# Depthwise convolution on two engines: GpSimd makes the taps of half of its tiles

## The chip, the cores and the metric

One core of a Trainium2 chip runs the whole program. The metric is device time in microseconds (us) of that core, the median of several executions. A core has five engines with their own instruction streams, which meet only through semaphores: PE (TensorE, matmuls), DVE (VectorE), ACT (ScalarE), POOL (GpSimd) and SP (SyncE, which here only starts DMAs). On-chip memory (SBUF) has 128 partitions; matmuls write to PSUM, 8 banks of 128 x 512 float32.

## The reference

Two transformer-like blocks over 256 tokens of width 1024, batch 1, all in float32. The first block has a layer whose mixer is a state space branch beside a neighbourhood attention, then an MLP, an mLSTM layer and a second MLP; the second block mixes three branches, then cross attention and a gated MLP. Every product multiplies the 256 tokens by weights that are read once. The part that the change touches is the first step of the state space branch, over 1536 channels (1024 for x, 256 each for B and C):

```python
proj = h @ w_in
z, xbc, dt_raw, qkv = jnp.split(proj, [s1, s2, s3], axis=-1)
...
xbc = jax.nn.silu(centred_dwconv(xbc, conv_w, conv_b))      # 5 taps, one filter per channel
xs, bm, cm = jnp.split(xbc, [SSD_WIDTH, SSD_WIDTH + SSD_GROUPS * SSD_STATE], axis=-1)
```

## The kernel before, in words

**Products.** The stream of weights comes from device memory in chunks of 128 x 2048 float32 (1 MB), through a ring of 7 slots that SP fills. For each chunk ACT rounds the weights to a high part (`split_hi`, L1382, into one of 3 buffers `w_hi`), DVE subtracts to get the low part in place (`split_lo`, L1393), and PE makes three passes (L1058: high x high, high weights x low source, low weights x high source). A group is 512 columns of output, two chunks at 1024 input rows, and goes to one pair of PSUM banks. When it is complete, ACT takes one bank and DVE the other. `in0` is the first product; its groups 0, 1 and 2 are the 1536 channels of the convolution (B and C first, then x), groups 3 and 4 are q, then k, z and v.

**Woven work.** Each engine's program is a Python generator. `Woven` runs the main product one quarter of a chunk at a time, and after each quarter lets side threads advance to a step given by `paced` tables. So the order of instructions on each engine is fixed when the program is built; nothing is reordered at run time. DVE has another side job in these stages, the guests: products of one vector with weights (the modulation `cond @ ada_w`), a multiply-add of 128 x 512 per row of tiles (L1200), whose sums PE then turns by four small matmuls (L1019). PE waits in order for the guest's last multiply-add before it goes on with the product.

**The convolution.** Channels lie on partitions, 12 tiles of 128 channels, tokens along the free dimension. `xp` holds the projection with two columns of padding at either side, `xc` the result. For each of the three groups of 4 tiles: ACT makes the first tap and the bias (`scalar`, L2202, 4 instructions, mark `first_tap`); DVE makes the other four taps of the 4 tiles, 16 instructions of the form `xc = xp[shifted] * w + xc` (`vector`, L2254, mark `convolved`), one tap after the other with a wait on its own steps between taps; ACT then applies Silu to the 4 tiles in one instruction (L2213, mark `silu_in`). In ACT's stream a Silu is followed by what the product needs: taking a group out of PSUM (L1991, L1998), splitting the next chunk (L1382), the first taps of the next group (L2202), and the high part of the running sums of the step sizes (L2065) that DVE's L2102 waits for.

**Readers of the convolution.** PE's L2140 (the product of B and C) reads the tiles of group 0, L2154 (transposes of x) those of groups 1 and 2. `silu_in` releases them.

**GpSimd.** In this stage POOL starts two DMAs (L594, L596) and then is idle until the next stages. It computes only in the second block: 16 times the four instructions L3207, L3208, L3210 (tensor times a scalar, 128 x 256) and L3212 (difference of two tensors, 128 x 256) for the phases of the S5 branch, and L3514 and L3519 (two tensors, 128 x 1024).

**Memory.** `e` is a ring of three buffers of 768 columns for the decays of the scan, used after the convolution. Before that `tmp`, its first 5 x 256 columns, holds the step sizes.

Of the kernel before, what the change touches and what calls it, by code (L numbers as in the profile page):

```python
# [300 lines left out]
class Mark:  # L301


    def __init__(self, sem, before):
        self.sem, self.before = sem, before
# [170 lines left out]
class Stage:  # L476
# [11 lines left out]
    def vector(self, dve, st):  # L488
        pass

    def gpsimd(self, pool, st):
        pass
# [1620 lines left out]
class Ssd(Stage):  # L2113
# [5 lines left out]

    def __init__(self, k, xp, xc, xt, cb, cs4, bias, tmp, e, in0):
        super().__init__(k)
        self.xp, self.xc, self.xt, self.cb, self.cs4, self.bias = xp, xc, xt, cb, cs4, bias
        self.tmp, self.e, self.first, self.narrow_in = tmp, e, in0.first_group, in0.narrow_in()
        self.m = {n: k.mark(n, c) for n, c in (
            ("biased", 1), ("log_in", 1), ("rates_in", 1), ("steps_in", 1), ("log_steps_in", 1), ("sums_in", 2),
            ("sums_hi", 1), ("sums_lo", 1), ("offsets_in", 1), ("offsets_turned", 1), ("offsets_taken", 1),
            ("first_tap", 3), ("convolved", 3), ("silu_in", 3), ("cb_in", 2), ("cb_taken", 2), ("x_turned", 4), ("x_taken", 4),
            ("decay_args", 2 * NH), ("decays_in", 2 * NH), ("weights_in", NH), ("head_out", NH), ("head_taken", NH // 2))}  # L2130

    def tensor(self, pe):
# [62 lines left out]
    def scalar(self, act, st):  # L2195
        k, m = self.k, self.m
        for n in range(3):
            at = 4 * ((n + 2) % 3)
            act.wait_ge(k.act_took, k.act_groups[self.first + n + 1])
            act.wait_ge(k.dve_took, k.dve_groups[self.first + n + 1])  # L2200
            for j in range(at, at + 4):
                ins = act.activation(self.xc[:, j, :], self.xp[:, j, 0:TOK], ACT.Identity,  # L2202
                                     scale=k.par("conv_w")[:, j:j + 1], bias=k.par("conv_b")[:, j:j + 1])
            ins.then_inc(m["first_tap"].sem, 1)
            yield
            if n == 2:
                for g in range(2):
                    act.wait_ge(*m["cb_in"].at(g + 1))
                    act.activation(self.cb[:, g, :], k.ps[:, 4 + g, :], ACT.Identity).then_inc(m["cb_taken"].sem, 1)
            for _ in range(4):  # L2210
                yield
            act.wait_ge(*m["convolved"].at(n + 1))
            act.activation(self.xc[:, at:at + 4, :], self.xc[:, at:at + 4, :], ACT.Silu).then_inc(m["silu_in"].sem, 1)  # L2213
            yield
            if n == 0:
                yield
        for half in range(2):
            for t in range(TT):
                act.wait_ge(*m["x_turned"].at(2 * half + t + 1))
                act.activation(self.xt[:, t, 512 * half:512 * half + 512], k.ps[:, 4 + t, :], ACT.Identity) \  # L2220
                   .then_inc(m["x_taken"].sem, 1)
            yield
        act.wait_ge(*m["offsets_taken"].at(1))
        for h in range(NH):
            e = self.e[:, h % 3, :]
            act.wait_ge(*m["decay_args"].at(2 * h + 1))
            if h >= 3:
                act.wait_ge(*m["head_out"].at(h - 2))
            c = h
            act.activation(e[:, 0:TOK], k.ps[:, 4, 0:TOK], ACT.Exp, bias=self.bias[:, 0, c:c + 1])  # L2230
            act.activation(e[:, 3 * P:4 * P], k.ps[:, 4, TOK:3 * P], ACT.Exp, bias=self.bias[:, 1, c:c + 1]) \
               .then_inc(m["decays_in"].sem, 1)
            yield
            act.wait_ge(*m["decay_args"].at(2 * h + 2))
            c = 64 + h
            act.activation(e[:, 4 * P:5 * P], k.ps[:, 5, 0:P], ACT.Exp, bias=self.bias[:, 0, c:c + 1])
            act.activation(e[:, 2 * P:3 * P], k.ps[:, 5, P:2 * P], ACT.Exp, bias=self.bias[:, 1, c:c + 1])
            act.activation(e[:, 5 * P:6 * P], k.ps[:, 5, 2 * P:3 * P], ACT.Exp, bias=self.bias[:, 1, c:c + 1]) \
               .then_inc(m["decays_in"].sem, 1)
            yield  # L2240
        yield

    def vector(self, dve, st):
        k, m = self.k, self.m
        for n in range(3):
            at = 4 * ((n + 2) % 3)
            for tap in range(5):
                if tap == 1:
                    dve.wait_ge(*m["first_tap"].at(n + 1))
                elif tap > 1:  # L2250
                    st.wait()
                for j in range(at, at + 4) if tap else ():
                    src, w = self.xp[:, j, tap:tap + TOK], k.par("conv_w")[:, 12 * tap + j:12 * tap + j + 1]
                    ins = dve.scalar_tensor_tensor(self.xc[:, j, :], src, w, self.xc[:, j, :], ALU.mult, ALU.add)  # L2254
                    if tap < 4 or j < at + 3:
                        st(ins)
                    else:
                        ins.then_inc(m["convolved"].sem, 1)
                yield
            yield  # L2260
            if n == 0:
                yield
        yield
        yield

        def weigh(h):
            e = self.e[:, h % 3, :]
            dve.wait_ge(*m["decays_in"].at(2 * h + 2))
            both = e[:, 0:6 * P].rearrange("p (a c) -> p a c", c=P)
            st(dve.tensor_tensor(both[:, 0:4:3, :], both[:, 0:4:3, :], both[:, 4:6, :], ALU.add))  # L2270
            st.wait()
            dve.tensor_tensor(e[:, 0:2 * TOK], e[:, 0:2 * TOK], self.cb[:, h // 8, :], ALU.mult) \
               .then_inc(m["weights_in"].sem, 1)

        def take(p):
            dve.wait_ge(*m["head_out"].at(2 * p + 2))
            dve.scalar_tensor_tensor(self.xc[:, p, :], self.xc[:, p, :], k.par("d_skip")[:, p:p + 1],
                                     k.ps[:, 6, 0:TOK], ALU.mult, ALU.add).then_inc(m["head_taken"].sem, 1)

        dve.wait_ge(*m["cb_taken"].at(2))  # L2280
        for h in range(NH):
            yield
            weigh(h)
            if h >= 2 and h % 2 == 0:
                take(h // 2 - 1)
            yield
        take(NH // 2 - 1)
        yield
# [2075 lines left out]
def all_stages(k, bias, kept, kept_hi):  # L4364
# [53 lines left out]
    mem = MemGroups(k, mem_turn, mem_rates, kept_hi, kept, mem_his, mem_lo, region(k, at_m).take(TT, CN))  # L4418
    tables = BiasLoad(k, table, bias, mem_turn, mem_rates)
    in0 = in0_stage(k, xp, xc, zs, qT, kT, v, z_in, ada_take(k, mods), first_norm, mem_turn.stored)  # L4420
    ssd = Ssd(k, xp, xc, xt, cb, cs4, biases, tmp, e, in0)
    norm = SsdNorm(k, xc[:, 0:KD, :], zs, ring2(at_z, KD, TOK, True), ring2(at_x, KD, TOK, True), rows, in0, z_in)
    na = Neighbours(k, lambda h, t: qT[64 * (h % 2):64 * (h % 2) + 64, h // 2, t * P:(t + 1) * P],
                    lambda h: kT[64 * (h % 2):64 * (h % 2) + 64, h // 2, :],
# [157 lines left out]
```

## Time and profile before

| | |
|---|---|
| median of 3 runs | 1630.98 us (1630.41 to 1633.61) |
| the profiled execution | 1631.24 us, span of its profile 1629.4 us |
| mean granted TensorE clock | 0.974 of full speed |
| PE busy, PE weight loads | 1529.9 us (94%), 1316.0 us |
| DVE busy | 1149.6 us (71%) |
| ACT busy | 789.2 us (48%) |
| POOL busy | 83.6 us (5%) |

The span is the time from the first to the last instruction of one profiled execution. "Busy" counts the time in which an engine had an instruction in work, also if that instruction waited for data or for a port. Shares over the whole span say little of one stage; the rows further down are taken from the stage that the change touches, about 70 to 130 us after the start.

### The profile page before, as it was taken

What the parts mean: (1) busy time and instruction counts of PE and PEld (TensorE: products, weight loads), DVE (VectorE), ACT (ScalarE), POOL (GpSimd) and SP (SyncE); (2) the same over time, 40 slices, a digit from 0 to 9 for tenths busy, and PEclk for the clock granted to TensorE, in tenths of its full rate; (3) what the DMA queues carried; (4) which work ended last, traced back from release to release, by engine and by line L of the source; (5) the groups of instructions that cost most, each with busy time, mean ns of one, the idle gap of its engine ahead of it and who ended that gap; (6) DMA issues with size and microseconds to landing.
All of it is one profiled execution on the core that took longest, in us unless ns stands there. A gap on an engine that the chain in (4) does not pass through costs nothing.

```text
span 1629.4 us, 23049 instructions
## 1 busy us (share of the span) xinstructions
PE 1529.9 (94%) x9240; PEld 1316.0 (81%) x9240; DVE 1149.6 (71%) x1812; ACT 789.2 (48%) x1078; POOL 83.6 (5%) x82
## 2 busy tenths in 40 slices
PE   8789998989999999999999999889998899999998
PEld 8779876679988888887899888756774778789987
DVE  4896775589877766776787567999963775466653
ACT  3645645454433546444554435656533734444442
POOL 0000000000000000000000002940020000000000
PEclk7889999999999999999999999999999999999999
DMA  9854523468777654335566555323321434145551
GB/s 389 318 220 185 215 85 136 144 225 318 283 280 288 243 169 145 131 128 194 200 240 233 181 195 206 130 104 111 125 103 75 181 129 155 59 172 184 181 190 68
DMA packets 42377, 298.10 MB, mean 183 GB/s; under 512 B 4640, under 2 KB 4896, under 8 KB 7328
## 3 DMA queue, kind: packets, MB, share of 16 engines
q1 hardware_dynamic: 39840, 283.00, 47.3%
q0 software_dynamic: 1568, 8.39, 1.4%
q10 hardware_dynamic: 864, 5.24, 0.9%
q8 instruction: 75, 1.23, 0.3%
q14 instruction: 30, 0.25, 0.0%
HBM read 292.42 MB, written 4.19 MB: 182 GB/s over the span
## 4 chain that ended last, share of the span: by engine, by line
PE 46%; DVE 22%; PEld 14%; issue 8%; ACT 7%; DMA 1%; POOL 1%; PEldq 1%; ACTq 0%; DVEq 0%; SPq 0%; POOLq 0%
PE ps L1050 16%; PE ps L1058 15%; PEld ps L1050 8%; DVE ring_at_lo L1393 7%; PEld ps L1058 5%; ACT w_hi L1382 3%; PE ps L1099 2%; DVE arena_at L1200 2%; DMA ring_at<-stream 1%; DVE arena_at L2254 1%; PE ps L2688 1%; PE ps L1274 1%; DVE arena_at L3255 1%; PE ps L546 1%; DVE arena_at L3264 1%
## 5 line engine op out<-in xcount | busy, mean ns | idle before, releaser
L1393 DVE TENSOR_TENSOR ring_at_lo<-ring_at,w_hi 128x2048 fp32r<-128x2048 f32 (+1 forms) x218 | 496.2, 2278 | 173.6 <-ACT w_hi L1382 173.1
L1382 ACT ACTIVATE w_hi<-ring_at 128x2048 fp32r<-128x2048 f32 (+1 forms) x218 | 413.7, 1902 | 193.9 <-PE ps L1050 134.0
L1050 PE MATMUL ps<-w_hi,arena_at_lo 128*128 128x512 f32 x1104 | 304.5, 397 | 1.9 <-DVEq L4504 0.8
L1058 PE MATMUL ps<-h_hi,w_hi 128*128 128x256 f32 x1440 | 244.3, 293 | 8.5 <-ACT w_hi L1382 3.4
L1050 PEld LDWEIGHTS ps<-w_hi,arena_at_lo 128*128 128x128 f32 x1104 | 204.3, 188 | 49.6 <-issue 3.0
L1058 PE MATMUL ps<-hT_at_lo,w_hi 128*128 128x256 f32 x1440 | 232.7, 285 | 0.0
L1058 PE MATMUL ps<-h_hi,ring_at_lo 128*128 128x256 f32 x1440 | 227.0, 280 | 0.0
L1058 PEld LDWEIGHTS ps<-h_hi,w_hi 128*128 128x128 f32 x1440 | 202.5, 194 | 15.8 <-issue 10.9
L1058 PEld LDWEIGHTS ps<-hT_at_lo,w_hi 128*128 128x128 f32 x1440 | 201.6, 193 | 0.0
L1058 PEld LDWEIGHTS ps<-h_hi,ring_at_lo 128*128 128x128 f32 x1440 | 194.7, 191 | 0.0
L1050 PE MATMUL ps<-ring_at_lo,arena_at_lo 128*128 128x512 f32 x552 | 172.1, 393 | 0.0
L1050 PE MATMUL ps<-w_hi,h_hi 128*128 128x512 f32 x368 | 124.5, 419 | 0.0
L1050 PEld LDWEIGHTS ps<-ring_at_lo,arena_at_lo 128*128 128x128 f32 x552 | 103.7, 188 | 24.3
L1050 PE MATMUL ps<-w_hi,hT_at_lo 128*128 128x512 f32 x368 | 116.0, 397 | 0.0
L1050 PE MATMUL ps<-ring_at_lo,h_hi 128*128 128x512 f32 x368 | 116.0, 396 | 0.0
L1200 DVE SCALAR_TENSOR_TENSOR arena_at<-ring_at,cond,arena_at 128x512 f32<-128x512 f32 x140 | 104.8, 748 | 3.7 <-DVE arena_at L1200 0.5
L1050 PEld LDWEIGHTS ps<-w_hi,hT_at_lo 128*128 128x128 f32 x368 | 70.3, 191 | 16.2
L1050 PEld LDWEIGHTS ps<-ring_at_lo,h_hi 128*128 128x128 f32 x368 | 69.6, 189 | 16.1
L1050 PEld LDWEIGHTS ps<-w_hi,h_hi 128*128 128x128 f32 x368 | 65.6, 191 | 19.5 <-issue 8.7
L546 PE MATMUL ps<-con 128*128 128x256 f32 x134 | 34.9, 412 | 8.3 <-DMA con<-consts 4.4
L546 PEld LDWEIGHTS ps<-con 128*128 128x128 f32 x134 | 27.0, 206 | 14.3 <-DMA con<-consts 4.4
L1099 PE MATMUL ps<-w_hi,arena_at_lo 128*128 128x512 f32 x128 | 35.5, 399 | 2.5 <-DVEq L4504 1.6
(471 smaller groups left out, 1743.6 us busy)
## 6 DMA issues: line engine op xcount, KB each, us to landing
ring_at<-stream SPq DMA_DIRECT2D x266, 1024.0 KB, 4.8
arena_at_lo<-kept_hi POOLq DMA_DIRECT2D x4, 1024.0 KB, 7.0
arena_at<-bias ACTq DMA_DIRECT2D x4, 768.0 KB, 5.8
kept<-arena_at POOLq DMA_DIRECT2D x4, 512.0 KB, 4.6
arena_at<-kept ACTq DMA_DIRECT2D x2, 1024.0 KB, 7.6
x_res<-x SPq DMA_DIRECT2D x1, 1024.0 KB, 9.5
arena_at<-mem POOLq DMA_DIRECT2D x1, 1024.0 KB, 11.1
kept_hi<-arena_at_lo POOLq DMA_DIRECT2D x1, 1024.0 KB, 4.2
```

What stands on the lines that cost most here:

```text
L546: pe.matmul(k.ps[:, bank, 0:TOK], k.con("ident"), k.con("ones"), start=True, stop=True)
L1050: mm = pe.matmul(k.ps[:, bank + t, :], x_tile(f, slice(t * P, (t + 1) * P)), w, start=first and n == 0, stop=last and n == 2)
L1058: mm = pe.matmul(k.ps[:, bank + q // 2, (q % 2) * TOK:(q % 2 + 1) * TOK], w[:, q * P:(q + 1) * P], x, start=first and n == 0 and q % 2 == ...
L1099: mm = pe.matmul(k.ps[:, bank + t, :], x[:, f, t * P:(t + 1) * P], w, start=f == 0 and n == 0, stop=f == KD - 1 and n == 2)
L1200: ins = dve.scalar_tensor_tensor(acc, w, cond, acc, ALU.mult, ALU.add)
L1274: pe.matmul(k.ps[:, self.opening_bank(n), 2 * q:2 * q + 2], k.ring[:, c % RING, kk, q * P:(q + 1) * P], k.cond[:, CK * j + kk:CK * j + kk ...
L1382: act.activation(k.w_hi[:, s % HI, 0:n, :], k.ring[:, c % RING, 0:n, :], ACT.Identity).then_inc(k.hi_done, 1)
L1393: dve.tensor_tensor(k.w_lo[:, c % RING, 0:n, :], k.ring[:, c % RING, 0:n, :], k.w_hi[:, s % HI, 0:n, :].bitcast(F32), ALU.subtract).then_i ...
L2254: ins = dve.scalar_tensor_tensor(self.xc[:, j, :], src, w, self.xc[:, j, :], ALU.mult, ALU.add)
L2688: mm = pe.matmul(k.ps[:, 6 + t, 0:MDV + 2], a, b, start=j == 0, stop=j == len(parts) - 1)
L3255: dve.tensor_tensor_scan(self.g[:, at], mag, a[:, at], 0.0, ALU.mult, ALU.add) \
L3264: dve.tensor_tensor(halves(self.b2[:, i % 3, :]), halves(self.g)[:, ::-1, :], halves(self.sn[:, i % 3, :])[:, ::-1, :], ALU.mult).then_inc ...
```

## The change

DVE makes taps 1 to 4 of the first two tiles of each group only. POOL makes those of the other two: it makes each product by `tensor_scalar` into a buffer `taps` (two tiles of 128 x 256), waits for both, and adds both to `xc` by one `tensor_tensor` of 128 x 512. `taps` lies in `e` behind `tmp`. ACT's Silu waits for both engines.

```diff
@@ Ssd
             ("first_tap", 3), ("convolved", 3), ("taps_by_pool", 36), ...
@@ Ssd.scalar
             act.wait_ge(*m["convolved"].at(n + 1))
+            act.wait_ge(*m["taps_by_pool"].at(12 * n + 12))
             act.activation(self.xc[:, at:at + 4, :], self.xc[:, at:at + 4, :], ACT.Silu).then_inc(m["silu_in"].sem, 1)
@@ Ssd.gpsimd
+    def gpsimd(self, pool, st):
+        k, m = self.k, self.m
+        for n in range(3):
+            at = 4 * ((n + 2) % 3)
+            pool.wait_ge(*m["first_tap"].at(n + 1))
+            for tap in range(1, 5):
+                done = 12 * n + 3 * tap - 3
+                if done:
+                    pool.wait_ge(*m["taps_by_pool"].at(done))
+                for j in (at + 2, at + 3):
+                    src, w = self.xp[:, j, tap:tap + TOK], k.par("conv_w")[:, 12 * tap + j:12 * tap + j + 1]
+                    pool.tensor_scalar(self.taps[:, j - at - 2, :], src, w, 1.0, ALU.mult, ALU.mult) \
+                        .then_inc(m["taps_by_pool"].sem, 1)
+                pool.wait_ge(*m["taps_by_pool"].at(done + 2))
+                pool.tensor_tensor(self.xc[:, at + 2:at + 4, :], self.xc[:, at + 2:at + 4, :], self.taps, ALU.add) \
+                    .then_inc(m["taps_by_pool"].sem, 1)
@@ Ssd.vector
-                for j in range(at, at + 4) if tap else ():
+                for j in range(at, at + 2) if tap else ():
                     src, w = self.xp[:, j, tap:tap + TOK], k.par("conv_w")[:, 12 * tap + j:12 * tap + j + 1]
                     ins = dve.scalar_tensor_tensor(self.xc[:, j, :], src, w, self.xc[:, j, :], ALU.mult, ALU.add)
-                    if tap < 4 or j < at + 3:
+                    if tap < 4 or j < at + 1:
                         st(ins)
@@ all_stages
-    ssd = Ssd(k, xp, xc, xt, cb, cs4, biases, tmp, e, in0)
+    ssd = Ssd(k, xp, xc, xt, cb, cs4, biases, tmp, e, in0, region(k, at_e + 5 * TOK).take(2, TOK))
```

Line numbers shift by 19 behind the new function: DVE's taps are L2273 in the changed kernel. POOL's new stream, from the second DMA on (the first tap of group 0 and part of the second; the pattern repeats 12 times):

```order
7 L596 DMA kept_hi<-arena_at_lo 128x2048 [waits turned_hi]
8 L2256 ISA
9 L2256 TENSOR_SCALAR arena_at<-arena_at,par 128x256 [waits first_tap]
10 L2256 TENSOR_SCALAR arena_at<-arena_at,par 128x256
11 L2259 TENSOR_TENSOR arena_at<-arena_at 128x512 [waits taps_by_pool]
12 L2256 TENSOR_SCALAR arena_at<-arena_at,par 128x256 [waits taps_by_pool]
```

Each addition waits for the products before it, and each tap's first product for the addition before it. ACT's stream around the first two Silus, before (L2213) and in the changed kernel (L2215):

```order
53 L2213 ACT_TABLE_LOAD
54 L2213 ACTIVATE arena_at<-arena_at 128x1024 [waits convolved]
55 L1382 ACTIVATE w_hi<-ring_at 128x2048 [waits chunk_used,chunk_loaded5]
56 L2202 ACTIVATE arena_at<-arena_at,par 128x256 [waits dve_took_group,act_took_group]
57 L2202 ACTIVATE arena_at<-arena_at,par 128x256 x3
```

```order
53 L2215 ACT_TABLE_LOAD [waits taps_by_pool]
54 L2215 ACTIVATE arena_at<-arena_at 128x1024 [waits convolved]
55 L1382 ACTIVATE w_hi<-ring_at 128x2048 [waits chunk_used,chunk_loaded5]
56 L2203 ACTIVATE arena_at<-arena_at,par 128x256 [waits dve_took_group,act_took_group]
57 L2203 ACTIVATE arena_at<-arena_at,par 128x256 x3
58 L1382 ACTIVATE w_hi<-ring_at 128x2048 [waits chunk_used,chunk_loaded6]
59 L2215 ACTIVATE arena_at<-arena_at 128x1024 [waits taps_by_pool,convolved]
60 L1991 ACTIVATE arena_at<-ps 128x2x256 [waits chunk_used]
61 L2065 ACTIVATE arena_at_lo<-arena_at 128x512 [waits sums_in]
```

The order on ACT is the same; the load of Silu's table, which had no wait, now stands behind the wait for POOL. On DVE the order around the third group's last taps, before and now (only the count in a tap differs):

```order
97 L2254 SCALAR_TENSOR_TENSOR arena_at<-arena_at,par 128x256 x4
98 L1200 SCALAR_TENSOR_TENSOR arena_at<-ring_at,cond,arena_at 128x512
99 L1393 TENSOR_TENSOR ring_at_lo<-ring_at,w_hi 128x2048
100 L1200 SCALAR_TENSOR_TENSOR arena_at<-ring_at,cond,arena_at 128x512
101 L2002 TENSOR_SCALAR arena_at<-ps 128x512
```

```order
97 L2273 SCALAR_TENSOR_TENSOR arena_at<-arena_at,par 128x256 x2
98 L1200 SCALAR_TENSOR_TENSOR arena_at<-ring_at,cond,arena_at 128x512
99 L1393 TENSOR_TENSOR ring_at_lo<-ring_at,w_hi 128x2048
100 L1200 SCALAR_TENSOR_TENSOR arena_at<-ring_at,cond,arena_at 128x512
101 L2002 TENSOR_SCALAR arena_at<-ps 128x512
```

The `L1200` at 100 is the guest's last step, for which PE's L1019 waits.

## Rows read from the trace of the kernel before

**Rows 1.** Page, part 1: busy us (share of the span) xinstructions.

```profile
PE 1529.9 (94%) x9240; PEld 1316.0 (81%) x9240; DVE 1149.6 (71%) x1812; ACT 789.2 (48%) x1078; POOL 83.6 (5%) x82
```

**Rows 2.** Windows: PE, PEld, DVE, ACT, POOL busy (x), PEclk, DMA share, GB/s.

```profile
72.00:119.00 47.00, 39.49 (x297) 38.92 (x296) 46.42 (x84) 23.02 (x26) 0.00 (x0) 0.90 0.63 236
119.00:170.00 51.00, 50.63 (x383) 45.80 (x384) 36.13 (x49) 28.99 (x62) 0.00 (x0) 0.95 0.47 170
```

**Rows 3.** Groups by line, 71.8 to 119.2 us: xcount | busy us, mean ns | idle.

```profile
L2254 DVE SCALAR_TENSOR_TENSOR arena_at<-arena_at,par 128x256 f32<-128x256 f32 x48 | 20.0, 478 | 0.1
L1393 DVE TENSOR_TENSOR ring_at_lo<-ring_at,w_hi 128x2048 fp32r<-128x2048 f32 x6 | 13.7, 2286 | 0.7 <-ACT w_hi L1382 0.6
```

**Rows 4.** Timeline of DVE: start us, us, engine, line, op, [idle before].

```profile
84.57 2.31 DVE L1200 SCALAR_TENSOR_TENSOR arena_at<-ring_at,cond,arena_at 128x512 f32<-128x512 f32 x3
86.98 2.29 DVE L1393 TENSOR_TENSOR ring_at_lo<-ring_at,w_hi 128x2048 fp32r<-128x2048 f32 x1
93.25 5.09 DVE L2254 SCALAR_TENSOR_TENSOR arena_at<-arena_at,par 128x256 f32<-128x256 f32 x12
101.84 1.40 DVE L2102 TENSOR_TENSOR arena_at_lo<-arena_at,arena_at_lo 32x512 fp32r<-32x512 f32 x2
105.07 1.67 DVE L2254 SCALAR_TENSOR_TENSOR arena_at<-arena_at,par 128x256 f32<-128x256 f32 x4
```

**Rows 5.** Timeline of ACT, first taps, Silus and what stands behind them.

```profile
69.78 2.06 ACT L2202 ACTIVATE arena_at<-arena_at,par 128x256 f32<-128x256 f32 x4
80.96 1.28 ACT L2213 ACT_TABLE_LOAD   x1
84.08 1.07 ACT L2213 ACTIVATE arena_at<-arena_at 128x1024 f32<-128x1024 f32 x1 [1.84 <-DVE arena_at L2254]
85.05 1.90 ACT L1382 ACTIVATE w_hi<-ring_at 128x2048 fp32r<-128x2048 f32 x1
98.38 1.06 ACT L2213 ACTIVATE arena_at<-arena_at 128x1024 f32<-128x1024 f32 x1 [7.67 <-DVE arena_at L2254]
99.82 0.62 ACT L2065 ACTIVATE arena_at_lo<-arena_at 128x512 fp32r<-128x512 f32 x1
101.51 2.08 ACT L2202 ACTIVATE arena_at<-arena_at,par 128x256 f32<-128x256 f32 x4 [1.07 <-DVE arena_at L1995]
115.70 1.06 ACT L2213 ACTIVATE arena_at<-arena_at 128x1024 f32<-128x1024 f32 x1 [7.28 <-DVE arena_at L2254]
```

**Rows 6.** Timeline of PE, the two waits for DVE and the second transposes.

```profile
90.08 1.59 PE L1019 MATMUL ps<-ones,arena_at 128*128 128x2 f32 x8 [1.64 <-DVE arena_at L1200]
119.34 1.83 PE L1019 MATMUL ps<-ones,arena_at 128*128 128x2 f32 x8 [6.21 <-DVE arena_at L1200]
126.41 1.04 PE L2154 MATMUL ps<-con,arena_at 128*128 128x128 f32 x8
```

**Rows 7.** Groups by line, POOL, whole span: xcount | busy us, mean ns.

```profile
L3208 POOL TENSOR_SCALAR arena_at<-con,arena_at 128x256 f32<-128x256 f32 x16 | 22.7, 1417 | 0.0
L3207 POOL TENSOR_SCALAR arena_at<-con,arena_at 128x256 f32<-128x256 f32 x16 | 15.8, 988 | 4.7 <-ACT arena_at L3186 3.4
L3212 POOL TENSOR_TENSOR arena_at<-arena_at 128x256 f32<-128x256 f32 x16 | 18.3, 1144 | 1.3
```

**Rows 8.** Instructions of one line: ns min/median/max, first and last start.

```profile
L3207 POOL TENSOR_SCALAR arena_at<-con,arena_at x16: 474/732/2614, 1010.3 to 1080.4; 128x256 f32<-128x256 f32 x16
L3212 POOL TENSOR_TENSOR arena_at<-arena_at x16: 727/986/2649, 1018.5 to 1082.3; 128x256 f32<-128x256 f32 x16
L3514 POOL TENSOR_TENSOR arena_at<-arena_at x2: 1889/2858/3826, 1202.3 to 1206.1; 128x1024 f32<-128x1024 f32 x2
```

**Rows 9.** The same of a DVE line, from 1009 to 1085 us.

```profile
L3246 DVE TENSOR_TENSOR arena_at<-arena_at x9: 659/898/1162, 1026.0 to 1082.7; 128x512 f32<-128x512 f32 x9
```

**Rows 10.** Timelines of POOL and DVE around 1035 us.

```profile
1034.91 2.65 POOL L3212 TENSOR_TENSOR arena_at<-arena_at 128x256 f32<-128x256 f32 x1
1034.48 2.48 DVE L1393 TENSOR_TENSOR ring_at_lo<-ring_at,w_hi 128x2048 fp32r<-128x2048 f32 x1
```

More of the change, by code:

```diff
@@ L2113, with __init__ @@
 class Ssd(Stage):
-    def __init__(self, k, xp, xc, xt, cb, cs4, bias, tmp, e, in0):
+    def __init__(self, k, xp, xc, xt, cb, cs4, bias, tmp, e, in0, taps):
         super().__init__(k)
+        self.taps = taps
         self.xp, self.xc, self.xt, self.cb, self.cs4, self.bias = xp, xc, xt, cb, cs4, bias
@@ L2128, in __init__ @@
             ("sums_hi", 1), ("sums_lo", 1), ("offsets_in", 1), ("offsets_turned", 1), ("offsets_taken", 1),
-            ("first_tap", 3), ("convolved", 3), ("silu_in", 3), ("cb_in", 2), ("cb_taken", 2), ("x_turned", 4), ("x_taken", 4),
+            ("first_tap", 3), ("convolved", 3), ("taps_by_pool", 36), ("silu_in", 3), ("cb_in", 2), ("cb_taken", 2), ("x_turned", 4), ("x_taken", 4),
             ("decay_args", 2 * NH), ("decays_in", 2 * NH), ("weights_in", NH), ("head_out", NH), ("head_taken", NH // 2))}
```

## The prediction

> **What bounds the kernel now.** I read the page's busy times first: PE is busy for 94% of the span, POOL for 5% [rows 1]. That makes POOL look free, and says nothing of the 50 us in which the convolution runs. So the next view is busy time by stretch: from 72 to 119 us DVE is busy for 46.4 of 47 us, PE only for 39.5 and ACT for 23.0; from 119 us on PE is busy for 50.6 of 51 us and DVE for 36.1 [rows 2]. DVE sets the pace first, PE afterwards, and PE's two idle times in the first stretch, 1.64 us before 90.08 and 6.21 us before 119.34, both end with DVE's L1200 [rows 6]. The chain of waits says the same in order of time: it runs along DVE up to the guest's last step and crosses to PE at 119.3 us. What DVE does there is in the groups by line: 48 taps (20.0 us), 6 low splits (13.7 us) [rows 3], and between them guest steps (L1200). All three read two tensors from SBUF.
>
> ACT is not the bound there, but it has little room. It waits 1.84, 7.67 and 7.28 us for DVE before the three Silus [rows 5], and what stands behind the first two is wanted almost at once: DVE's split at 86.98 follows ACT's L1382, which ends at 85.05 + 1.90 = 86.95 [rows 4, 5], with DVE done with its guest steps at 86.88; DVE's L2102 at 101.84 needs ACT's L2065, which ends at 99.82 + 0.62 = 100.44 [rows 4, 5].
>
> **What is taken from DVE.** Twelve taps in a row take 5.09 us, 0.42 each [rows 4]. 24 of 48 go: 24 x 0.42 = 10.1 us, 3.4 us in each group. The waits between taps stay.
>
> **What POOL's work takes by itself.** Per group and tap two products and an addition of 128 x 512. A product of 128 x 256 takes 0.47 us at least, an addition 0.73 at 256 columns and 1.89 at 1024 [rows 8], so 1.51 ns a column and 1.11 us at 512. With the two handovers a tap takes 2.2 us, a group 8.8. But while DVE works beside it POOL's instructions are longer: means of 0.99 and 1.42 us for the products, 1.14 for the addition of 256 [rows 7], so some 1.5 for one of 512. Then a tap takes 4.1 us and a group 16.4. What these instructions waited for can be read at 1035 us: POOL's addition begins at 1034.91 while DVE's split runs from 1034.48 to 1036.96, takes 2.65 us in place of 0.73, and ends 0.6 us behind the split [rows 10]. POOL's instruction is in work but held until DVE's ends. Here DVE is as full of such instructions as there, but a tap (0.42 us) stands in front of POOL for less time than S5's instructions (0.66). I take **3.8 us a tap, 15.2 a group**, near the upper end, and keep 2.2 and 4.5 as bounds. The library call before POOL's first product I cost at nothing: the same call stood before L3207, whose longest instance, 2.61 us, is explained by one split in front.
>
> **What POOL's work costs DVE.** The other direction is in the row of L3246, which reads two SBUF tensors: 0.66 us undisturbed, 0.90 typically beside POOL's products, 1.16 at most beside an addition of 256 columns [rows 9]. The same split as above takes 2.48 us, against 2.28 alone, a product of POOL having been ahead of it [rows 3, 10]. So a product holds DVE up for 0.24 us, an addition of 256 for 0.50, and one of 512 by the slope above for 0.50 + 0.39 = 0.89. Per tap 1.37 us, 12 taps 16.4 us if every instruction meets such an instruction of DVE. That is more than the 10.1 us that DVE sheds. The Trainium skill (SBUF — State Buffer, "SBUF: two separate sides") calls the pair of ports that the two engines share an exclusive lock that the winner has "for the whole instruction". The trace agrees that there is no sharing, but not on the length: DVE lost 0.24 us to instructions that take 0.47. By the page's rule a tap would cost DVE 0.47 + 0.47 + 1.11 = 2.05 us; I go by the rows.
>
> **Group by group.** *First group.* The first taps end at 69.78 + 2.06 = 71.84 us, and the Silu ran 12.2 us later, at 84.08 [rows 5]. POOL is done at 71.84 + 15.2 = 87.0. In front of this Silu stands a load of its table, 1.28 us, which lay in ACT's wait at 80.96 [rows 5] and now comes behind the wait for POOL. So the Silu starts at 88.3, 4.2 us late, and with it the split, DVE's L1393, the guest step that PE waits for, and the first taps of the next group, which end at 93.1 in place of 86.95 + 2.06 = 89.0. DVE alone would have been at that split at 86.9 - 3.4 + 5.5 = 89.0, before ACT's 91.2: ACT sets the time.
> *Second group.* POOL: 93.1 + 15.2 = 108.3, against a Silu at 98.38. L2065 ended 2.06 us behind the Silu's start [rows 5], so it ends at 110.3, where DVE needed it at 101.84: DVE, which has been through its taps for long, stands still and resumes **8.5 us late**. The first taps of the third group come at about 112.4 (the 1.07 us that ACT waited for DVE in front of them is gone), DVE's own taps at 105.07 + 8.5 = 113.6.
> *Third group.* From there to the guest's last step DVE sheds 3.4 us. POOL gets through some three taps meanwhile; since part of its instructions meet an instruction on PSUM or none, I charge 2.5 taps, 3.4 us, with 0 and 5.5 as bounds. So the guest's last step and PE's L1019 come 8.5 us late. POOL itself ends near 128, the Silu near 129; PE's second L2154, its reader, stood at 126.41 [rows 6] and now stands at 135: hidden, and it stays so up to 21 us a group.
>
> Sum: +4.2 (first group) + 4.3 (second) - 3.4 + 3.4 = **+8.5 us**. From 119 us on PE has no idle time to take it in [rows 2], and a ring of 7 chunks can't save up more than it holds, so the shift goes through to the end. The profiled execution took 1631.24 us, 0.26 above the median of the runs: 1639.7 against it, **1639.5 us** as a median. Of the clock: PE was granted 0.90 of full speed from 72 to 119 us and 0.95 after [rows 2]; it idles before L1019 in both kernels, so I add no term, but 2 us to either side.
>
> **Rivals.**
> *DVE's relief wins (0.09).* If POOL's reads and DVE's did not hold each other up, POOL would need 8.8 us a group, less than the 12.2, 9.5 and 12.2 us from first taps to Silu. DVE would shed 10.1 us, but PE has no idle time between 91.5 and 113 us, so of the first two groups' relief only PE's 1.64 us come back, and of the third's all 3.4: -5.0, 1626.0 us. For it: PE's waits all end with DVE, and POOL is empty. Against it: rows 9 and 10.
> *A draw on DVE (0.14).* POOL's additions hold the ports no longer than for 256 columns, and its chain stays inside ACT's waits. DVE alone decides: -10.1 + 24 x 0.24 + 12 x 0.50 = +1.7, with the table's load up to +3.0: 1632.7 to 1634. Against it: the second group has only 9.5 us, and POOL's means don't fit into that.
> *The whole instruction is held (0.12).* Then a tap costs DVE 0.68 us more, 8.2 us in all, of which two thirds fall on time that counts: 8.5 + 5.5, 1645 us. This is what the rule of the page above would do here.
> The decisive point between faster and slower is POOL's time for a group: over some 10 us the second Silu is late, and L2065 hands that to DVE.
>
> **How the numbers follow.** My forecast (1634.5 to 1643) has 0.62, the rivals 0.09, 0.14 and 0.12; 0.03 is left for POOL at over 4.5 us a tap, beyond 1646. About 0.2% (3.3 us) can be told from no change. The draw is mostly within that and gives 0.11 of "same"; slower has 0.80. The range from 1632 to 1646 takes in the draw, the forecast and the whole-instruction case, and leaves out the faster one.
>
> **What would show it.** Right: POOL's 36 instructions take about 45 us, the products 0.8 to 1.4 us and the additions 1.4 to 1.6; DVE's taps are longer than 0.48 us in the mean; ACT's waits before the Silus end with POOL; the table's load starts only when POOL is done; DVE has idle time before L2102 that ends with ACT's L2065, and PE's L1019 stands near 128. Wrong: POOL's products near 0.47 us and additions near 1.1 (the first rival), or DVE without idle time before L2102 (the draw).

## The result and the profile after

| | before | after |
|---|---|---|
| median, us | 1631.22 (20 runs, 1626.67 to 1633.77) | 1635.53 (20 runs, 1632.79 to 1643.55) |
| after / before | | 1.0039, 95% interval 1.0028 to 1.0051 |
| profiled execution, us | 1631.24, span 1629.4 | 1632.88, span 1631.0 |

The change costs 0.39%, that is 6.4 us, 4.6 to 8.3 us by the interval. It is slower, as forecast, inside the range and 4 us below the number. The medians differ by only 4.3 us, since eight of the 20 executions after lie at 1639.8 to 1643.6 us, apart from the other twelve (up to 1636.7) and at a slightly lower mean granted clock.

The page's busy times after, against [rows 1]: POOL has 36 instructions and 36 us more, DVE has 24 instructions fewer and is busy for 6.6 us longer.

```profile
PE 1524.1 (93%) x9237; PEld 1312.3 (80%) x9240; DVE 1156.2 (71%) x1788; ACT 789.6 (48%) x1078; POOL 120.0 (7%) x118
```

Groups of instructions by line, the shapes kept apart, DVE of the changed kernel from 71 to 122 us (count | busy us, mean ns | idle before). L2273 are the taps, L1200 the guest's steps.

```profile
L2273 DVE SCALAR_TENSOR_TENSOR arena_at<-arena_at,par 128x256 f32<-128x256 f32 x24 | 22.9, 992 | 0.1
L1393 DVE TENSOR_TENSOR ring_at_lo<-ring_at,w_hi 128x2048 fp32r<-128x2048 f32 x5 | 11.4, 2284 | 1.4 <-ACT w_hi L1382 1.4
L1200 DVE SCALAR_TENSOR_TENSOR arena_at<-ring_at,cond,arena_at 128x512 f32<-128x512 f32 x12 | 10.4, 867 | 0.1
```

**24 taps now keep DVE busy for longer (22.9 us) than 48 did (20.0) [rows 3].** The work was halved and the time per tap doubled. The low splits have not changed (2.28 us). The two groups of POOL over the stretch, products and additions:

```profile
L2256 POOL TENSOR_SCALAR arena_at<-arena_at,par 128x256 f32<-128x256 f32 x24 | 20.4, 859 | 19.9 <-ACT arena_at L2203 19.0
L2259 POOL TENSOR_TENSOR arena_at<-arena_at 128x512 f32<-128x512 f32 x12 | 16.9, 1410 | 1.0
```

PE's two waits for the guest, which stood at 90.08 and 119.34 with 1.64 and 6.21 us of idle time [rows 6]:

```profile
93.06 1.84 PE L1019 MATMUL ps<-ones,arena_at 128*128 128x2 f32 x8 [4.49 <-DVE arena_at L1200]
126.69 1.84 PE L1019 MATMUL ps<-ones,arena_at 128*128 128x2 f32 x8 [9.14 <-DVE arena_at L1200]
```

ACT: the first taps of the second and third group (L2203), and the three Silus (L2215) with the load of their table, to be compared with [rows 5]:

```profile
85.55 1.28 ACT L2215 ACT_TABLE_LOAD   x1 [4.47 <-POOL arena_at L2259]
86.85 1.06 ACT L2215 ACTIVATE arena_at<-arena_at 128x1024 f32<-128x1024 f32 x1
89.62 2.06 ACT L2203 ACTIVATE arena_at<-arena_at,par 128x256 f32<-128x256 f32 x4
103.23 1.06 ACT L2215 ACTIVATE arena_at<-arena_at 128x1024 f32<-128x1024 f32 x1 [9.75 <-DVE arena_at L2273]
106.36 2.08 ACT L2203 ACTIVATE arena_at<-arena_at,par 128x256 f32<-128x256 f32 x4 [1.07 <-DVE arena_at L1995]
123.05 1.06 ACT L2215 ACTIVATE arena_at<-arena_at 128x1024 f32<-128x1024 f32 x1 [9.77 <-DVE arena_at L2273]
```

Only the first Silu waits for POOL. The other two wait for DVE, as before.

How DVE loses its time is best read in the third group. The timeline of DVE in the changed kernel ("..." stands for lines left out; the last line is the guest's last step, behind POOL's end):

```profile
117.13 0.96 DVE L1200 SCALAR_TENSOR_TENSOR arena_at<-ring_at,cond,arena_at 128x512 f32<-128x512 f32 x1
118.02 2.10 DVE L2273 SCALAR_TENSOR_TENSOR arena_at<-arena_at,par 128x256 f32<-128x256 f32 x2
120.04 0.96 DVE L1200 SCALAR_TENSOR_TENSOR arena_at<-ring_at,cond,arena_at 128x512 f32<-128x512 f32 x1
120.92 2.10 DVE L2273 SCALAR_TENSOR_TENSOR arena_at<-arena_at,par 128x256 f32<-128x256 f32 x2
...
125.80 0.74 DVE L1200 SCALAR_TENSOR_TENSOR arena_at<-ring_at,cond,arena_at 128x512 f32<-128x512 f32 x1
```

The timeline of POOL over the same microseconds:

```profile
117.03 1.42 POOL L2256 TENSOR_SCALAR arena_at<-arena_at,par 128x256 f32<-128x256 f32 x2
118.52 1.30 POOL L2259 TENSOR_TENSOR arena_at<-arena_at 128x512 f32<-128x512 f32 x1
119.93 1.42 POOL L2256 TENSOR_SCALAR arena_at<-arena_at,par 128x256 f32<-128x256 f32 x2
121.43 1.31 POOL L2259 TENSOR_TENSOR arena_at<-arena_at 128x512 f32<-128x512 f32 x1
```

The two engines go step by step: three instructions of POOL fit three of DVE. The guest's step takes 0.96 us in place of 0.74, and the two taps 2.10 in place of some 0.84 (0.42 each [rows 4]). The line for all taps says how the 2.10 divides (minimum, median and maximum in ns):

```profile
L2273 DVE SCALAR_TENSOR_TENSOR arena_at<-arena_at,par x24: 472/696/1516, 74.4 to 121.5; 128x256 f32<-128x256 f32 x24
```

One tap of a pair waits behind a product (696 ns, 0.22 more than 0.478), the other behind an addition (1516 ns, 1.04 more). The guest's step in front of them waits behind the other product, 0.22 us. So one tap on POOL, of two tiles, costs DVE 0.22 + 0.22 + 1.04 = 1.48 us in this group, 5.9 us for four, and takes 8 x 0.42 = 3.4 us off it: 2.5 us net.

### The profile page after: what moved, and what is told of

Read it like the earlier page. It is cut to its first block, busy times and chain, and to the rows that moved or that the text cites. A ratio compares the mean times of both kernels' runs of the same rounds, so it can differ in the third digit from the quotient of the medians.

```text
span 1631.0 us, 23063 instructions
## 1 busy us (share of the span) xinstructions
PE 1524.1 (93%) x9237; PEld 1312.3 (80%) x9240; DVE 1156.2 (71%) x1788; ACT 789.6 (48%) x1078; POOL 120.0 (7%) x118
## 4 chain that ended last, share of the span: by engine, by line
PE 47%; DVE 22%; PEld 14%; issue 8%; ACT 7%; DMA 1%; POOL 1%; PEldq 1%; ACTq 0%; DVEq 0%; SPq 0%; POOLq 0%
PE ps L1050 17%; PE ps L1058 15%; PEld ps L1050 8%; DVE ring_at_lo L1393 7%; PEld ps L1058 5%; ACT w_hi L1382 3%; DVE arena_at L1200 2%; PE ps L1099 2%; DVE arena_at L2273 1%; PE ps L2707 1%; PE ps L1274 1%; DMA ring_at<-stream 1%; PE ps L3177 1%; DVE arena_at L3274 1%; PE ps L546 1%
## 5 line engine op out<-in xcount | busy, mean ns | idle before, releaser
L1050 PE MATMUL ps<-w_hi,arena_at_lo 128*128 128x512 f32 x1104 | 304.5, 397 | 1.8 <-DVEq L4523 0.8
L1058 PEld LDWEIGHTS ps<-h_hi,w_hi 128*128 128x128 f32 x1440 | 201.1, 193 | 16.9 <-issue 11.6
L1200 DVE SCALAR_TENSOR_TENSOR arena_at<-ring_at,cond,arena_at 128x512 f32<-128x512 f32 x140 | 106.3, 759 | 3.4
L1019 PE MATMUL ps<-ones,arena_at 128*128 128x2 f32 x160 | 22.2, 261 | 21.6 <-DVE arena_at L1200 21.6
## 6 DMA issues: line engine op xcount, KB each, us to landing
arena_at<-mem POOLq DMA_DIRECT2D x1, 1024.0 KB, 11.1
```

Source lines behind the costliest of these rows:

```text
L1019: mm = pe.matmul(k.ps[:, ADA, 2 * q:2 * q + 2], k.guest_acc[:, n % 2, q * P:(q + 1) * P], k.ones[:, :], start=True, stop=True)
L1050: mm = pe.matmul(k.ps[:, bank + t, :], x_tile(f, slice(t * P, (t + 1) * P)), w, start=first and n == 0, stop=last and n == 2)
L1058: mm = pe.matmul(k.ps[:, bank + q // 2, (q % 2) * TOK:(q % 2 + 1) * TOK], w[:, q * P:(q + 1) * P], x, start=first and n == 0 and q % 2 == ...
L1200: ins = dve.scalar_tensor_tensor(acc, w, cond, acc, ALU.mult, ALU.add)
```

## The experiments

The first two take the change apart: the relief without POOL's work, and POOL's work without the relief. Two more take the Silus' waits away and halve POOL's share. Two give POOL one kind of instruction only, and the rest ask where the lost time goes and how to avoid it. The edits are shown against the changed kernel, those of `delay`, `guest_at_9` and `guests_at_6_9` against the kernel before; "..." marks what is left out. "Shift" is always the start of PE's second L1019 against 119.34 us. The profiles start the stretch up to 0.3 us apart (the first taps of ACT at 69.47 us in the changed kernel, 69.78 before, 69.92 at the latest), so shifts are good to some 0.3 us. Ratios are to the kernel before, run beside each set on the same chip (medians 1629.81, 1631.08 and 1630.41 us for the three sets).

### `relief_only`: what DVE sheds, by itself

```diff
-            act.wait_ge(*m["taps_by_pool"].at(12 * n + 12))
...
-    def gpsimd(self, pool, st):
...
```

> Left out: taps 1 to 4 of the last two tiles of each group; nobody makes them. DVE has 24 taps, POOL none. This prices DVE's relief alone. PE's second wait for the guest (L1019) ended at 119.3 us before and at 126.7 us in the changed kernel. Ports theory (each POOL instruction holds up DVE's, and DVE is the bound): without POOL the relief of 10.1 us is cut by PE's own pace to about 5: L1019 near 114.5, the time about 5 us below the kernel before. Waits theory (the loss comes from ACT waiting for POOL's chain and the table's load behind it): the same here, so this run only fixes what is to be gained.

Measured: 1623.68 us, ratio 0.996 (0.9943 to 0.9977), which is worth 3.7 to 9.3 us less. The second L1019 stands at 111.51 us:

```profile
111.51 1.49 PE L1019 MATMUL ps<-ones,arena_at 128*128 128x2 f32 x8 [3.00 <-DVE arena_at L1200]
```

A shift of -7.8 us, not the -5 that I expected. The relief is real and it reaches PE. What the changed kernel lost is thus 7.8 + 7.35 = 15.2 us against this one.

### `beside`: POOL's work without any relief

```diff
-            act.wait_ge(*m["taps_by_pool"].at(12 * n + 12))
...
-                pool.tensor_tensor(self.xc[:, at + 2:at + 4, :], self.xc[:, at + 2:at + 4, :], self.taps, ALU.add) \
+                pool.tensor_tensor(self.taps, self.xp[:, at + 2:at + 4, 0:TOK], self.taps, ALU.add) \
...
-                for j in range(at, at + 2) if tap else ():
+                for j in range(at, at + 4) if tap else ():
```

> DVE makes all 48 taps as before. POOL does its 24 products and 12 additions beside it, into a buffer that nothing reads, and no Silu waits for it (only ACT's later writes over the same memory do). Ports theory: DVE loses 1.3 to 1.4 us for each of the 12 taps that POOL works on, 15 us or somewhat more: L1019 near 134, the time 12 to 16 us above before. Waits theory: nothing waits for POOL, so L1019 stays at 119 to 120 and the time is that of before.

Measured: 1650.2 us, ratio 1.012 (1.0099 to 1.0141). No Silu waits for POOL's 36 instructions, and yet PE's waits for DVE between 70 and 170 us are three times those of the kernel before, which were 7.9 us in all. The two largest groups (us in total, times, longest):

```profile
PE ps L1019 <- DVE arena_at L1200: 14.2, 2, 8.9
PE ps L1058 <- DVE ring_at_lo L1393: 7.9, 3, 3.5
```

The shift is 136.21 - 119.34 = +16.9 us, where I expected 15 or somewhat more. The time rose by 16.1 to 23 us, above the 12 to 16 that I expected; what came on top of the shift was not traced. DVE does exactly the work of before, so all of it is time in which its instructions were in work and held:

```profile
L2273 DVE SCALAR_TENSOR_TENSOR arena_at<-arena_at,par 128x256 f32<-128x256 f32 x48 | 30.5, 693 | 0.1
L1393 DVE TENSOR_TENSOR ring_at_lo<-ring_at,w_hi 128x2048 fp32r<-128x2048 f32 x7 | 17.0, 2435 | 0.7 <-ACT w_hi L1382 0.6
L1200 DVE SCALAR_TENSOR_TENSOR arena_at<-ring_at,cond,arena_at 128x512 f32<-128x512 f32 x14 | 13.2, 943 | 0.1
```

Against the kernel before the taps take 10.5 us more, the guest steps 14 x 0.2 = 2.8 and the splits 7 x 0.15 = 1.1; most of the remaining 2.5 us is in L2084 and L2089, which are some 1.0 us longer each. The forecast's term, 16.4 us for 12 taps of POOL, is confirmed as a size.

### `unwaited`: is it the wait?

The first two edits of `beside` without the third: DVE keeps its two tiles.

```diff
-            act.wait_ge(*m["taps_by_pool"].at(12 * n + 12))
...
-                pool.tensor_tensor(self.xc[:, at + 2:at + 4, :], self.xc[:, at + 2:at + 4, :], self.taps, ALU.add) \
+                pool.tensor_tensor(self.taps, self.xp[:, at + 2:at + 4, 0:TOK], self.taps, ALU.add) \
```

> As the changed kernel, but POOL adds into a buffer of its own and no Silu waits for it (only ACT's later writes over the same memory do); so the taps 1 to 4 of two tiles of each group are missing in the result. Ports theory: DVE is held up as before, and only the 0.76 us that it waited behind the table's load come back: L1019 at 125.7 to 126.2, the time within 1 us of the changed kernel. Waits theory: most of the loss goes: L1019 at 121 or earlier, the time at least 5 us below the changed kernel.

Measured: 1634.86 us, ratio 1.0044 (1.0026 to 1.0061), second L1019 at 126.22. Against 126.69 in the changed kernel the waits are worth 0.5 us. What I had made the carrier of the loss in the first two groups carries next to nothing.

### `one_tile`: half of POOL's share

```diff
-                for j in (at + 2, at + 3):
+                for j in (at + 3,):
...
-                pool.tensor_tensor(self.xc[:, at + 2:at + 4, :], self.xc[:, at + 2:at + 4, :], self.taps, ALU.add) \
+                pool.tensor_tensor(self.xc[:, at + 3, :], self.xc[:, at + 3, :], self.taps[:, 0, :], ALU.add) \
...
-                for j in range(at, at + 2) if tap else ():
+                for j in range(at, at + 3) if tap else ():
```

> POOL makes the taps of one tile of four in place of two: 12 products and 12 additions of 128 x 256. DVE has 36 taps. Ports theory: DVE sheds 12 x 0.42 = 5.0 us and loses 12 x (0.22 + 0.64) = 10.3, the addition's hold taken from the 1.03 us at 512 columns less 256 columns of 1.5 ns: L1019 at 124 to 125, the time 4 to 6 us above before. Waits theory: POOL's chain is then some 7 us a group and inside ACT's waits, only the relief is left: L1019 at 116 or earlier, the time below before.

Measured: 1634.72 us, ratio 1.0026 (1.0011 to 1.004), second L1019 at 122.36, a shift of +3.0 us, less than the 5 that I expected. Half the share, less than half the loss, and still a loss: 12 taps go from DVE (12 x 0.42 = 5.0 us), so the hold is 8.0 us, 0.67 for each product and addition of 256 columns. That is more than the 0.42 which they save.

### `products_only` and `additions_only`: which instruction holds

Both leave DVE's 48 taps and give POOL one kind of instruction, its output going to a buffer that nothing reads.

```diff
 (products_only)
-                pool.wait_ge(*m["taps_by_pool"].at(done + 2))
-                pool.tensor_tensor(self.xc[:, at + 2:at + 4, :], self.xc[:, at + 2:at + 4, :], self.taps, ALU.add) \
-                    .then_inc(m["taps_by_pool"].sem, 1)
 (additions_only: in place of products and addition)
+                pool.tensor_tensor(self.taps, self.xp[:, at + 2:at + 4, 0:TOK], self.xp[:, at + 2:at + 4, tap:tap + TOK], ALU.add) \
```

> VectorE makes all 48 taps as before, GpSimd makes the 24 products of 128 x 256 beside them into a buffer that nothing reads, no addition, and no Silu waits for it; the output is complete. It splits the hold that `beside` showed by instruction. If a product holds VectorE for 0.24 us (the forecast's term), PE's second wait for the guest ends 24 x 0.24 = 5.8 us late, at 125, and the kernel takes 5 to 7 us more. If VectorE waits out the whole instruction, 24 x 0.47 = 11.3 us, at 130.5. If the products cost nothing and only the additions do, it stays at 119.3 to 120.

> VectorE makes all 48 taps as before, GpSimd makes 12 additions of 128 x 512 beside them (two tiles of the projection, into a buffer that nothing reads), no product, and no Silu waits for it; the output is complete. If an addition holds VectorE for 0.89 us (the forecast's term), PE's second wait ends 12 x 0.89 = 10.7 us late, at 130, less what meets an instruction on PSUM; with the 1.03 us by which a tap was longer in the changed kernel, 12.4 us, at 131.5. If an addition holds no longer than one of 256 columns (0.50), 6 us, at 125. Together with `products_only` the shifts should add to that of `beside`, 16.9 us.

Measured: products 1638.03 us, ratio 1.0037 (1.002 to 1.0053), second L1019 at 124.08, shift +4.7 us; additions 1640.34 us, 1.0063 (1.0042 to 1.0085), at 128.41, shift +9.1 us. So a product holds DVE for 4.7 / 24 = **0.20 us**, an addition for 9.1 / 12 = **0.76 us** on average. The sum, 13.8 us, is 3.1 short of `beside`, where the kinds alternate; I had expected the two to add up to it. At the start of `additions_only` DVE's timeline shows three instructions behind one addition each:

```profile
72.14 0.81 DVE L1783 SCALAR_TENSOR_TENSOR arena_at<-arena_at,par 128x4 f32<-128x4 f32 x1
72.87 0.47 DVE L1197 TENSOR_SCALAR arena_at<-ring_at,cond 128x512 f32<-128x512 f32 x1
73.27 1.26 DVE L2082 SCALAR_TENSOR_TENSOR arena_at<-arena_at 128x256 f32<-128x256 f32 x1
74.56 1.01 DVE L2084 TENSOR_SCALAR arena_at<-arena_at 128x256 f32<-128x256 f32 x1
```

L1783, on 4 columns, takes 0.16 us alone and 0.81 here; L2082 0.42 and 1.26; L2084, which reads one tensor, 0.29 and 1.01. Each ends behind an addition of POOL (four of them follow one another from 71.76 us, 4.78 us in all), and L1197 between them has its 0.48 us.

### `delay`: the same shift without POOL

```diff
+DELAY = (6, 5, 5)
...
+                for _ in range(DELAY[n]) if tap == 4 else ():
+                    st.wait()
+                    st(dve.scalar_tensor_tensor(self.taps[:, 0, :], self.xp[:, at, 0:TOK], k.par("conv_w")[:, 0:1],
+                                                self.xp[:, at, 0:TOK], ALU.mult, ALU.add))
```

> The kernel before with 16 more multiply-adds of 128 x 256 on VectorE (6, 5 and 5 in the three groups, into a buffer that nothing reads), GpSimd empty, no new wait, output complete. 16 x 0.45 = 7.2 us more on VectorE, so PE's second wait for the guest ends at 126.5, as in the changed kernel, without any port contention. It asks why the changed kernel is only 4.3 us slower as a median with 7.3 us more at 126 us. If a shift of PE at 120 us is in part made up later whatever its cause, this kernel's median is 4 to 5 us above that of before too. If GpSimd's work gave something back, this one is 7 us slower and the changed one not.

Measured: 1638.73 us, ratio 1.0048 (1.0033 to 1.0063), second L1019 at 127.37, shift +8.0 us. The ratio is worth 5.4 to 10.3 us, 7.8 in the middle: a plain delay of DVE of that size goes through to the end. The changed kernel's (4.6 to 8.3 us for +7.35) agrees with it: there is no sign that POOL's work gave anything back, though the intervals would hide 2 us.

### `guest_at_9`: what takes the load off DVE's full stretch

```diff
-GUESTS = {"in0": [-1, -1, 0, 0, 2, 5, 8, 11, 14, 17], ...
+GUESTS = {"in0": [-1, -1, 0, 0, 2, 5, 9, 11, 14, 17], ...
```

> The kernel before with one number changed: the seventh guest of the first product is paced by group 9 instead of group 8, so that four of its multiply-adds move from before VectorE's low split at 116.25 us to behind 119, and PE's small matmuls for it come five quarters later. GpSimd is empty, the output complete. If VectorE's load from 72 to 119 us is what PE waits for, the split moves forward by 4 x 0.74 = 3.0 us, PE's idle time of 6.21 us shrinks to 2 to 3 us, and the kernel is 3 to 4 us faster than before, which is what taking the taps off VectorE could not do. Rival: the guest's end is then late for VectorE's or PE's next steps, and PE waits as long behind 125 us: no change.

Measured: **1624.21 us, ratio 0.9949 (0.9932 to 0.9967)**, faster than both kernels. PE's waits from 70 to 170 us:

```profile
PE ps L2154 <- ACT arena_at L2220: 2.3, 1, 2.3
PE ps L1019 <- DVE arena_at L1200: 1.2, 1, 1.2
```

The 6.21 us in front of the guest's turning are gone. The split of before's 116.25 us is at 114.28, 2.0 us earlier (3.0 expected); PE passes 119 us without a wait, and the splits from 134 to 580 us start 6.1 to 6.4 us earlier, the last one 9.1. The ratio is worth 5.4 to 11.1 us, and I had expected 3 to 4. The waits above are 3.5 us where the kernel before had 7.9, which gives 4.4 of the 6.3 us or so from 134 us on. The granted clock can account for the rest (72 to 119 and 119 to 170 us; columns as in [rows 2]):

```profile
72.00:119.00 47.00, 43.52 (x341) 42.96 (x341) 45.97 (x83) 24.70 (x30) 0.00 (x0) 0.94 0.63 232
119.00:170.00 51.00, 50.97 (x390) 45.01 (x389) 39.95 (x55) 31.48 (x66) 0.00 (x0) 0.97 0.60 227
```

PE was granted 0.94 of full speed up to 119 us where it had 0.90, and 0.97 after where it had 0.95 [rows 2]: 0.04 x 47 + 0.02 x 51 = 2.9 us, some of which falls behind the steps that were compared. Behind the wait at 90 us PE ran at the lower of its two levels (1.2 of 2.4 GHz), with 1.05 us for four matmuls in place of 0.64, until 94 us here and until 97 us in the kernel before.

### `after_guest_at_9`: the change on top of the better order

```diff
 (the changed kernel)
-GUESTS = {"in0": [-1, -1, 0, 0, 2, 5, 8, 11, 14, 17], ...
+GUESTS = {"in0": [-1, -1, 0, 0, 2, 5, 9, 11, 14, 17], ...
```

> The changed kernel (GpSimd makes half of the taps) with the seventh guest paced by group 9, as in `guest_at_9`; output complete. It asks whether the division of the taps would pay, or cost nothing, where PE does not wait for the guest. If holding VectorE is what costs, VectorE's steps up to the third Silu come 5 to 7 us later than in `guest_at_9` here too (that Silu from 113.7 to about 120 us), PE waits for ACT's copies behind it (2.3 us in `guest_at_9`, now 7 to 9), and the kernel is 5 to 6.5 us slower than `guest_at_9`, about level with the kernel before (1625 to 1631 against 1631). If the changed kernel's loss came from the guest's last step alone, it is within 2 us of `guest_at_9` (1624 to 1626).

Measured: 1635.73 us, ratio 1.0024 (1.0011 to 1.0038), some 0.75% or 12 us above `guest_at_9` by the ratios. I had expected 5 to 6.5 us and a time of 1625 to 1631: the loss is larger than forecast. The second transposes of x started at 117.71 us in `guest_at_9`, and here at 125.81:

```profile
125.81 1.94 PE L2155 MATMUL ps<-con,arena_at 128*128 128x128 f32 x8 [5.13 <-ACT arena_at L2222]
```

That is 8.1 us later, where I expected 5 to 7; the third Silu is at 121.84 against 113.73, also 8.1. Here the wait in front of it ends with POOL's last addition. One split met an addition and took 3.18 us:

```profile
110.62 3.18 DVE L1393 TENSOR_TENSOR ring_at_lo<-ring_at,w_hi 128x2048 fp32r<-128x2048 f32 x1 [0.70 <-ACT w_hi L1382]
```

PE was granted 0.93 of full speed from 119 to 170 us here, and 0.97 in `guest_at_9`, which is worth some 2 us; the rest of what came on top of the 8.1 us was not traced. The loss does not hang on the guest's last step.

### `guests_at_6_9`: one more guest moved

```diff
-GUESTS = {"in0": [-1, -1, 0, 0, 2, 5, 8, 11, 14, 17], ...
+GUESTS = {"in0": [-1, -1, 0, 0, 2, 6, 9, 11, 14, 17], ...
```

> `guest_at_9` with the sixth guest moved by one group as well (6 instead of 5), GpSimd empty, output complete. PE's wait of 1.2 us at 90.2 us should go, but that guest's multiply-adds then stand behind 90 us on VectorE, in front of the splits that PE needs up to 119. If VectorE is still full there, they push the third Silu, and PE gets its 1.2 us back as a longer wait behind 113 us: 1623 to 1626, level with `guest_at_9`. If there is room, 1 to 2 us faster.

Measured: 1626.36 us, ratio 0.9978 (0.9963 to 0.9992). By the ratios, each against its own set, that is 0.3% above `guest_at_9`, with intervals that overlap at their ends, so at best no gain. PE's wait for the moved guest, 1.2 us at 90 us, is now this:

```profile
101.25 1.84 PE L1019 MATMUL ps<-ones,arena_at 128*128 128x2 f32 x8 [7.20 <-DVE arena_at L1200]
```

Its steps went into a stretch of DVE that was full as well. I had expected the 1.2 us to come back as a longer wait behind 113 us, not a wait of 7 us at 101.

## Why the prediction was right in its direction, and where its steps failed

| start of | before | forecast | measured |
|---|---|---|---|
| first Silu | 84.08 | 88.3 | 86.85 |
| split at 86.98 | 86.98 | 91.2 | 89.74 |
| L2102 of DVE | 101.84 | 110.3 | 106.69 |
| PE's second L1019 | 119.34 | 127.8 | 126.69 |
| PE's second transposes | 126.41 | 135, hidden | 133.81, no wait |

**What is taken from DVE: right.** 10.1 us by count. `relief_only` brought 7.8 of them to PE's second L1019. The rival "DVE's relief wins" had counted only -5.0, with PE's idle time as its limit: too small.

**What POOL's work costs DVE: right in size, and this carried the result.** The term was 16.4 us. Count it back from the trace: the first group's split came 2.8 us late, 0.76 of which DVE waited for ACT; with the 3.4 us of relief the hold is 5.4 (the step's own 5.5, and its 89.0 us for DVE alone, where DVE was free at 89.74 - 0.76 = 88.98). L2102 came 2.1 us later still: 5.5. The last group added 2.5: 5.9. That is 16.8 us. By the experiments the product, priced at 0.24 us, holds 0.20 to 0.22; the addition, priced at 0.89, holds 0.76 where POOL makes only additions and 1.04 between products.

**What POOL's work takes by itself: too long.** 15.2 us a group; the groups took 13.8 (71.64 to 85.48), 11.1 and 14.2 us. The products came to 0.86 us in the mean, not up to 1.42, since a split stood in front of few of them.

**First group, "ACT sets the time": the right place, a third of the size.** The load of the table does come behind POOL's last addition, and DVE does wait: 0.76 us, not the 2.2 between 89.0 and 91.2.

```profile
89.74 2.29 DVE L1393 TENSOR_TENSOR ring_at_lo<-ring_at,w_hi 128x2048 fp32r<-128x2048 f32 x1 [0.76 <-ACT w_hi L1382]
```

**Second group, DVE "stands still and resumes 8.5 us late": wrong.** This is the step that failed. POOL's last addition of the group, DVE's last taps of it, and DVE's L2102, in the changed kernel:

```profile
101.59 1.32 POOL L2259 TENSOR_TENSOR arena_at<-arena_at 128x512 f32<-128x512 f32 x1
97.97 5.22 DVE L2273 SCALAR_TENSOR_TENSOR arena_at<-arena_at,par 128x256 f32<-128x256 f32 x6
106.69 1.40 DVE L2102 TENSOR_TENSOR arena_at_lo<-arena_at,arena_at_lo 32x512 fp32r<-32x512 f32 x2
```

DVE has no idle time before L2102, which is 4.85 us late and not 8.5. POOL was through its second group at 102.91, and the Silu behind it waited for DVE's taps until 103.23. DVE came late because it was held, not because it stood. The forecast ran POOL's chain and DVE's on separate clocks. In the trace the two engines wait for each other instruction by instruction, so a POOL that takes longer makes DVE's own taps end later too, and the chain through Silu and L2065 hardly gets ahead; `unwaited` puts all the Silus' waits together at 0.5 us. The forecast had named the sign for this: no idle time of DVE before L2102 means that DVE alone decides.

**Third group, "I charge 2.5 taps": too few.** All four taps of POOL fall in front of the guest's last step, each some 1.48 us: 5.9 us, not 3.4.

The two errors partly cancel, 4.85 in place of 8.5 and then +2.5 in place of 0, so +7.35 stands against +8.5. That the sum came so near is luck; the direction is not, since the price of POOL's work was right and exceeds the relief. The rival **"a draw on DVE"** had the mechanism and the wrong price for the addition (0.50). Its sum with the forecast's price of the ports is -10.1 + 16.4 = +6.3, and with the 0.76 us that DVE did wait +7.1.

Of the signs named ahead, the lengths of POOL's instructions (0.86 and 1.41 us), the longer taps and the table's load behind POOL came as said; POOL's total was 37 us, not 45, and two of the three Silus did not wait for it.

**The whole instruction is held: not so for the products.** A product holds DVE for 0.20 us and takes 0.48 at least itself. An addition of 128 x 512 takes 1.05 at least where POOL makes only additions, and holds DVE for 0.76 there on average, for 1.04 between the products of the changed kernel:

```profile
L2254 POOL TENSOR_TENSOR arena_at<-arena_at x12: 1045/1135/1588, 71.8 to 114.0; 128x512 f32<-128x512 f32 x12
```

The rule of the Trainium skill (SBUF — State Buffer, "SBUF: two separate sides") would have made `products_only` 11.3 us later; it was 4.7. For the longer addition the rule comes near: DVE loses 0.84 of 1.05 us where one instruction stands behind one addition, and practically all of it between products. Part of the difference can be read in the timelines above: DVE's pair of taps ends at 120.12 us, 0.3 us behind the addition's end at 119.82, where a tap takes 0.48 alone. So about the last 0.2 us of POOL's recorded instruction no longer hold DVE. No run varied this alone, so its size stays an estimate from these rows. The runs show that POOL's instructions hold DVE's; that what is held is the pair of ports which both share is the prediction's reading, and no run separates it from another common path.

**From 126 us to the end.** The forecast passed the shift through 1:1, as `delay` did. In the profile of the changed kernel the low splits start 6.8 to 7.4 us late up to 580 us, 5.5 to 7.3 up to 1115 us, and the last one only 1.6 (1614.7 against 1613.1). The largest part of that difference arises between 1310 and 1400 us, where the clock differs, before and then after (columns as in [rows 2]):

```profile
1310.00:1400.00 90.00, 83.02 (x466) 71.56 (x465) 52.77 (x74) 36.03 (x53) 0.00 (x0) 0.94 0.37 128
```

```profile
1310.00:1400.00 90.00, 83.39 (x490) 71.94 (x489) 57.48 (x87) 37.58 (x57) 0.00 (x0) 1.00 0.37 132
```

PE was granted 0.94 of full speed before and 1.00 after, over 90 us: 0.06 x 90 = 5.4 us, in code that the change does not touch; the splits are 6.4 us late at its start and 1.6 at its end, 4.8 less. This lets one execution of the changed kernel end at 1632.88 us, 2.7 below its median. Why the clock fell in the one and not in the other was not settled.

## What to carry to other kernels

An engine at 5% is not free if its instructions hold up those of the one that is full: the price of moving an instruction is what it takes from the neighbour, and it has to be set against what the neighbour sheds. Here one tap of two tiles on GpSimd cost VectorE 1.4 us (16.8 for 12) and saved 0.84. And where one engine is full for 50 us and then has room, look first for work in that stretch that can wait: one number in a table gave 0.5%, where both divisions of the taps lost.

When two engines hold each other up instruction by instruction, don't run a clock for each and take the later: the slower one's delay is in the faster one's instructions already.

## What the runs showed of the hardware

- Busy time hides a hold. In `beside` DVE did the work of before and its 48 taps read 30.5 us in place of 20.0, with 0.1 us of idle time in front.
- POOL's hold falls on DVE instructions that read one tensor of SBUF too: L2084 takes 0.29 us alone, 1.01 in `additions_only` and 1.25 in the changed kernel.
- The length of DVE's own instruction matters little for the hold: one on 4 columns (L1783) lost 0.65 us to an addition, a split on 2048 columns 0.9 (3.18 against 2.28).
